# Early expert table and first expert weights in the routing block, and PE adding the gated rows in the last stage

## The reference, cut to what matters

```python
logits = (t @ w_router + b_router)
top_vals, top_idx = lax.top_k(logits, 4)
probs = jax.nn.softmax(top_vals)
order = argsort(flat_e)                       # token rows sorted by expert
gu = ragged_dot(xs, w_gu, group_sizes) + b_gu[e_sorted]
out = ragged_dot(act, w_down, group_sizes) + b_down[e_sorted]
ffn = einsum('tkd,tk->td', slots, probs)
x = layer_norm(DN_ALPHA * x + g2 * ffn, ln2_g, ln2_b)
```

## Time and profile before

| | us |
|---|---|
| runs of the kernel before (3) | 6109.48, 6113.31, 6122.75 |
| median | 6113.31 |
| profiled execution, its time | 6120.77 |
| profiled execution, its span | 6119.2 |
| PE busy in it | 5785.5 (95%) |
| DVE busy | 4270.6 (70%) |
| routing block, from DVE's first instruction (L1711) to its last (L1794) | 3089.6 to 3162.4 |
| experts, POOL's first copy to PE's last product | 3163.8 to 5999.5 |
| last stage, first DMA issue to the end of the span | 6011.2 to 6119.2 |

### The profile page before, as it was taken

The page is one execution under the profiler, slowest core; times in us unless marked ns, Lnnn a source line. Parts: engine busy times, 40 slices in busy tenths (PEclk is TensorE's granted clock), DMA queues, the critical chain, the costliest instruction groups (busy, mean ns, idle before and its releaser), DMA issues. The chain is left out here.

```text
span 6119.2 us, 78464 instructions
## 1 busy us (share of the span) xinstructions
PE 5785.5 (95%) x27512; PEld 4699.9 (77%) x27512; DVE 4270.6 (70%) x3430; ACT 3157.2 (52%) x2883; POOL 1033.3 (17%) x751
## 2 busy tenths in 40 slices
PE   5899999998999989998959999999999999999995
PEld 2688888886777768886748888888888888888882
DVE  3333300224566565554779999999999999999996
ACT  5222211003444444442337777777777777777772
POOL 1000000002333320001511111111111111111112
PEclk7899999999999999999969999999999999999997
DMA  5311212113444445554329553315468359532455
GB/s 224 119 72 72 79 72 74 46 41 102 132 137 133 136 159 186 183 187 149 128 117 357 170 187 120 120 31 199 150 218 328 123 210 408 212 93 58 139 189 186
DMA packets 298555, 924.56 MB, mean 151 GB/s; under 512 B 25808, under 2 KB 163280, under 8 KB 260368
## 3 DMA queue, kind: packets, MB, share of 16 engines
q1 hardware_dynamic: 207696, 701.59, 31.1%
q0 software_dynamic: 40800, 170.84, 9.9%
q10 hardware_dynamic: 49920, 50.34, 2.4%
HBM read 744.27 MB, written 178.54 MB: 151 GB/s over the span
## 5 line engine op out<-in xcount | busy, mean ns | idle before, releaser
L2012 DVE TENSOR_TENSOR moe_w_lo<-moe_w_gu,moe_w_hi 128x2048 fp32r<-128x2048 f32 x648 | 1441.0, 2287 | 3.0 <-ACT moe_w_hi L1958 3.0
L1958 ACT CAST moe_w_hi<-moe_w_gu 128x2048 fp32r<-128x2048 f32 x648 | 1238.7, 1912 | 378.0 <-PE moe_ps_gu L1901 191.4
L2018 DVE TENSOR_TENSOR moe_w_lo<-moe_w_dn,moe_w_hi 128x2048 fp32r<-128x2048 f32 x324 | 734.2, 2288 | 31.8 <-ACT moe_w_hi L1968 31.8
L1968 ACT CAST moe_w_hi<-moe_w_dn 128x2048 fp32r<-128x2048 f32 x324 | 620.2, 1915 | 256.2 <-PE moe_ps_gu L1901 256.2
L1901 PE MATMUL moe_ps_gu<-moe_w_hi,moe_hT_hi 128*128 128x512 f32 x2592 | 702.6, 393 | 12.3 <-DVE moe_w_lo L2012 12.3
L166 PE MATMUL prj_ps_p<-h_hi,prj_w_hi 128*128 128x512 f32 x1792 | 698.5, 390 | 15.7 <-DVE prj_w_lo L537 15.7
L166 PE MATMUL prj_ps_p<-h_hi,prj_w_lo 128*128 128x512 f32 x1792 | 698.1, 390 | 0.0
L166 PE MATMUL prj_ps_p<-h_lo,prj_w_hi 128*128 128x512 f32 x1792 | 698.1, 390 | 0.0
L1901 PE MATMUL moe_ps_gu<-moe_w_lo,moe_hT_hi 128*128 128x512 f32 x2592 | 694.4, 390 | 0.0
L1901 PE MATMUL moe_ps_gu<-moe_w_hi,moe_hT_lo 128*128 128x512 f32 x2592 | 694.0, 390 | 0.0
L1901 PEld LDWEIGHTS moe_ps_gu<-moe_w_lo,moe_hT_hi 128*128 128x128 f32 x2592 | 487.8, 188 | 101.8
(11 more groups left out here) (322 smaller groups left out, 9553.2 us busy)
## 6 DMA issues: line engine op xcount, KB each, us to landing
moe_w_gu<-in_w_gu_t SPq DMA_DIRECT2D x128, 2048.0 KB, 11.0
moe_w_dn<-in_w_down_t SPq DMA_DIRECT2D x64, 2048.0 KB, 9.6
rows_scratch<-prj_out POOLq DMA_DIRECT2D x48, 1024.0 KB, 4.4
brn_w<-in_w_branch_t SPq DMA_DIRECT2D x64, 768.0 KB, 6.8
prj_w<-in_w_in_t SPq DMA_DIRECT2D x80, 512.0 KB, 4.3
moe_b_gu<-b_gu_scratch SPq DMA_DIRECT2D x32, 1024.0 KB, 8.8
nin_w<-in_w_ada SPq DMA_DIRECT2D x24, 1024.0 KB, 8.0
rows_scratch<-ssd_out ACTq DMA_DIRECT2D x96, 256.0 KB, 2.9
```

Source lines behind the costliest of these rows:

```text
L1958: act.copy(w_hi[n % NB][:], raw(w_gu, n)).then_inc(gu_hi, 1)
L1968: act.copy(w_hi[(GU + n) % NB][:], raw(w_dn, n)).then_inc(dn_hi, 1)
L2012: dve.tensor_tensor(w_lo[n % NB][:], raw(w_gu, n), w_hi[n % NB][:].bitcast(F32), ALU.subtract).then_inc(gu_lo, 1)
L2018: dve.tensor_tensor(w_lo[b][:], raw(w_dn, n), w_hi[b][:].bitcast(F32), ALU.subtract).then_inc(dn_lo, 1)
```

## The change

It has two parts.

**In the routing block**: rank and counts are read where they lie in PSUM. The expert of each tile is worked out right behind `cum`: partition c counts the experts whose running sum is at most c (128x32), and PE turns that column into a row with the identity. `S.expert` is written before the picks, on one partition. SP, which had nothing to do in this block, reads the first expert and issues the four transfers of its gate and up weights there; `w_gu` and its semaphores are allocated ahead of the block, and `fetch_gu(0)` in the experts' block returns at once. The four products of `hot` become one of four times the size.

```diff
-                pe.wait_ge(iotas, 6)
+                pe.wait_ge(iotas, 7)
                 pe.wait_ge(chosen_ready, 1)
                 rhs = chosen[:].rearrange("p t e -> p (t e)")
                 pe.matmul(psR[:], strict[:], rhs, start=True, stop=True)
                 pe.matmul(psC[:], S.ones[:], rhs, start=True, stop=True).then_inc(ranked, 1)
+                pe.wait_ge(owned, 1)
+                pe.matmul(psE[0:1, 0:P], te_col[:], S.ident[:], start=True, stop=True).then_inc(owners, 1)
...
+
+            @block.sync
+            def _(sp):
+                sp.wait_ge(tabled, 1)
+                apart(sp, S)
+                first = sp.value_load(S.expert[0:1, 0:1], min_val=0, max_val=E - 1)
+                for c, dst in enumerate(S.w_gu):
+                    sp.dma_start(dst[:], A["w_gu_t"][bass.ds(first * GU_ROWS + c * P, P), :]).then_inc(S.gu_in[c], 16)
...
-                chain.step(dve.tensor_copy(rank[:].rearrange("p t e -> p (t e)"), psR[:]))
-                chain.step(dve.tensor_copy(count[:].rearrange("p t e -> p (t e)"), psC[:]))
                 chain.step(dve.memset(base[:, 0, :], 0.0))
                 for t in range(TT):
-                    chain.step(dve.tensor_tensor(base[:, t + 1, :], base[:, t, :], count[:, t, :], ALU.add))
+                    chain.step(dve.tensor_tensor(base[:, t + 1, :], base[:, t, :], psC[:, t * E:(t + 1) * E], ALU.add))
...
-                chain.step(dve.tensor_tensor(place[:], rank[:], base[:, 0:TT, :], ALU.add))
+                chain.step(dve.tensor_scalar(cmp[:], cum[a][:], iota_c[:, 0:1], None, ALU.is_le))
+                chain.step(dve.tensor_reduce(te_col[:], cmp[:], AX.X, ALU.add))
+                dve.tensor_scalar(te_col[:], te_col[:], float(E - 1), None, ALU.min).then_inc(owned, 1)
+                chain.step(dve.tensor_tensor(place[:], psR[:].rearrange("p (t e) -> p t e", e=E), base[:, 0:TT, :], ALU.add))
                 chain.step(dve.tensor_tensor(place[:], place[:], tiles[:].unsqueeze(1).to_broadcast([P, TT, E]), ALU.add))
-                for k in range(TOPK):
-                    chain.step(dve.tensor_tensor(hot[:, :, k, :], hot[:, :, k, :], place[:], ALU.mult))
+                dve.wait_ge(owners, 1)
+                chain.step(dve.tensor_copy(S.expert[0:1, :], psE[0:1, 0:MOE_COLS]))
+                dve.sem_inc(tabled, 1)
+                chain.step(dve.tensor_tensor(hot[:], hot[:], place[:].unsqueeze(2).to_broadcast([P, TT, TOPK, E]), ALU.mult))
...
-                chain.step(dve.tensor_tensor(cmp[:], iota_t[:].unsqueeze(2).to_broadcast([P, MOE_COLS, E]),
-                                             cum[a][:].unsqueeze(1).to_broadcast([P, MOE_COLS, E]), ALU.is_ge))
-                chain.step(dve.tensor_reduce(te[:], cmp[:], AX.X, ALU.add))
-                chain.step(dve.tensor_scalar(te[:], te[:], float(E - 1), None, ALU.min))
-                chain.step(dve.tensor_copy(S.expert[:], te[:]))
-
+                chain.step(dve.tensor_copy(te[:], psE[0:1, 0:MOE_COLS]))
                 chain.step(dve.memset(fresh[:, 0:1], 1.0))
                 chain.step(dve.tensor_tensor(fresh[:, 1:], te[:, 1:], te[:, :MOE_COLS - 1], ALU.not_equal))
-                chain.step(dve.tensor_copy(S.fresh[:], fresh[:]))
+                chain.step(dve.tensor_copy(S.fresh[0:1, :], fresh[:]))
...
-        w_gu = [sb(f"w_gu{k}", [P, CHUNK * U]) for k in range(GL)]
+        w_gu = S.w_gu
...
-        gu_in, dn_in = sems("moe_gu_in", GL), sems("moe_dn_in", DL)
+        gu_in, dn_in = S.gu_in, sems("moe_dn_in", DL)
...
                 def fetch_gu(i):
+                    if isinstance(i, int) and i == 0:
+                        return
                     fetch(i, [(w_gu[c], lambda e, c=c: A["w_gu_t"][bass.ds(e * GU_ROWS + c * P, P), :], gu_in[c],
                                gu_lo, GU * (i - 1) + CHUNK * (c + 1)) for c in range(GL)])
...
+        S.w_gu = [sb(f"w_gu{c}", [P, D * 2 * FF // GU_ROWS]) for c in range(GU_ROWS // P)]
+        S.gu_in = sems("gu_in", len(S.w_gu))
         route(nc, A, S, sem, sems)
         experts(nc, A, S, sem, sems)
         combine(nc, A, S, sem, sems, out)
```

```diff
-        psT = ps("dense", [E3, SEQ])
-        psB = [ps(f"rest{i}", [P, D]) for i in range(2)]
...
+        sums = ps("sums", [P, B * D])
+        psT = sums[0:E3, 2 * D:2 * D + SEQ]
+        psB = [sums[:, i * D:(i + 1) * D] for i in range(B)]
...
                 def load_x1(t):
                     wait(sp, rested, t - R + 1)
                     apart(sp, S)
-                    sp.dma_start(x1[t % R][:], S.x1_d[t * P:(t + 1) * P, :]).then_inc(x1_in[t % R], 16)
+                    sp.dma_start(x1[t % R][:], S.x1_d[t * P:(t + 1) * P, :]).then_inc(row_in[t % R], 16)
 
                 def load_acc(t):
-                    wait(sp, scaled, t - R + 1)
+                    wait(sp, taken, t - R + 1)
                     apart(sp, S)
-                    sp.dma_start(acc[t % R][:], S.sum_d[t * P:(t + 1) * P, :]).then_inc(acc_in[t % R], 16)
+                    sp.dma_start(acc[t % R][:], S.sum_d[t * P:(t + 1) * P, :]).then_inc(row_in[t % R], 16)
...
                 for t in range(TT):
-                    wait(pe, added, t - 1)
-                    pe.wait_ge(x1_in[t % R], 16 * (t // R + 1))
+                    if t == 2:
+                        pe.wait_ge(dense_ready, 2)
+                    wait(pe, normed, t - B + 1)
+                    pe.wait_ge(row_in[t % R], 32 * (t // R + 1))
                     for c in range(D // BANK):
                         cols = slice(c * BANK, (c + 1) * BANK)
-                        pe.matmul(psB[t % 2][:, cols], alpha[:], x1[t % R][:, cols], start=True, stop=False)
+                        last = pe.matmul(psB[t % B][:, cols], alpha[:], x1[t % R][:, cols], start=True, stop=False)
+                    last.then_inc(rested, 1)
+                    pe.wait_ge(gated, t + 1)
+                    for c in range(D // BANK):
+                        cols = slice(c * BANK, (c + 1) * BANK)
+                        last = pe.matmul(psB[t % B][:, cols], S.ident[:], acc[t % R][:, cols], start=False, stop=False)
+                    last.then_inc(taken, 1)
                     if t == 0:
                         pe.wait_ge(dense_ready, 2)
                         pe.wait_ge(bdn_ready, 3)
                     for c in range(D // BANK):
                         cols = slice(c * BANK, (c + 1) * BANK)
-                        last = pe.matmul(psB[t % 2][:, cols], d_part[:, t * P:(t + 1) * P], b_part[:, cols], start=False, stop=True)
-                    last.then_inc(rested, 1)
+                        pe.matmul(psB[t % B][:, cols], d_part[:, t * P:(t + 1) * P], b_part[:, cols], start=False, stop=True).then_inc(added, 1)
...
                 def normalise(t):
                     act.wait_ge(shifted, t + 1)
-                    act.activation(acc[t % R][:], acc[t % R][:], ACT.Identity, bias=nb[t % Y][:], scale=rs[t % Y][:]).then_inc(normed, 1)
+                    wait(act, stored[t % Y], 16 * (t // Y))
+                    act.activation(yo[t % Y][:], psB[t % B], ACT.Identity, bias=nb[t % Y][:], scale=rs[t % Y][:]).then_inc(normed, 1)
...
                 def gate(t):
-                    dve.wait_ge(acc_in[t % R], 16 * (t // R + 1))
+                    dve.wait_ge(row_in[t % R], 32 * (t // R + 1))
                     dve.tensor_tensor(acc[t % R][:], acc[t % R][:], g2[:], ALU.mult).then_inc(gated, 1)
 
                 def blend(t):
                     s = t % Y
-                    dve.wait_ge(gated, t + 1)
-                    dve.wait_ge(rested, t + 1)
-                    dve.tensor_tensor(acc[t % R][:], psB[t % 2][:], acc[t % R][:], ALU.add).then_inc(added, 1)
-                    dve.wait_ge(added, t + 1)
                     for half in range(2):
-                        dve.bn_stats(st[s][:, half, :], acc[t % R][:, half * BANK:(half + 1) * BANK]).then_inc(halves, 1)
+                        dve.wait_ge(added, 2 * t + half + 1)
+                        dve.bn_stats(st[s][:, half, :], psB[t % B][:, half * BANK:(half + 1) * BANK]).then_inc(halves, 1)
...
                 def scale(t):
                     dve.wait_ge(normed, t + 1)
-                    wait(dve, stored[t % Y], 16 * (t // Y))
                     if t == 0:
                         dve.wait_ge(ln_in, 32)
-                    dve.tensor_tensor(yo[t % Y][:], acc[t % R][:], lg[:], ALU.mult).then_inc(scaled, 1)
+                    dve.tensor_tensor(yo[t % Y][:], yo[t % Y][:], lg[:], ALU.mult).then_inc(scaled, 1)
...
                 gate(0)
+                gate(1)
                 for t in range(TT + 1):
                     if t < TT:
                         blend(t)
-                    if t + 1 < TT:
-                        gate(t + 1)
+                    if t + 2 < TT:
+                        gate(t + 2)
                     if t < TT:
                         invert(t)
                     if t > 0:
```

24 lines of the change are left out of this document (14 added, 10 removed).

## The result

| | before | changed |
|---|---|---|
| median of the runs, us | 6116.2 (6 runs, 6109.48 to 6122.75) | 6096.19 (6 runs, 6088.15 to 6098.51) |
| profiled execution, its time | 6120.77 | 6095.71 |
| its span | 6119.2 | 6094.0 |

The ratio of the runs is 0.9965, with a 95% interval of 0.9955 to 0.9975: the changed kernel is faster by 20.0 us, where 21.1 were predicted. (Before was run again beside the changed kernel, so its median is a little above the 6113.3 of the first three runs.)

A forecast was written before the change was run, and what follows sets the result against it. PE was busy 95% of the span, so only places where it waits could give. Gains of 7.6 + 6.2 + 7.3 = 21.1 us took the profiled 6120.8 to 6099.7, or the median 6113.3 to 6092.2; range 6077 to 6103.

The forecast's parts named there:

- Routing block: DVE's chain in the routing block: 9.6 us removed, 2.0 added, net gain 7.6 us, bounds 7.0 and 9.
- Start of the experts: First gather, issue to turned rows, takes 6 us with the weights transferred early; gain 6.2 us, bounds 0 and 8.1.
- Rival B: Start of the experts: gather stays late because bias and down weights replace gate and up weights; total gain 15, 6098; chance 0.11.
- Last stage: Addition taken off DVE, gating held until POOL ends: 4.94 us per tile; gain 7.3 us, bounds 0 and 20.
- 0.4 us of DVE's wait: Last stage, each tile: this wait for POOL becomes visible as a long gating of some 1.8 us.
- Rival A: Last stage: POOL does not hold up the gating, tile 4.06 us; stage gains some 20, total 34, 6079; chance 0.07.
- the last two tiles: Last stage: no gating left; about 3.7 instead of 5.3 us for one, about 0.9 gained on the last; together 2.5.
- the twelve tiles: Last stage: tiles of the regular form take 4.94 us each, a gain of 0.37 apiece, 4.4 us together.
- both are covered, with 0.7 us and a tenth to spare: Last stage: PE's 3.9 to 4.2 us per tile and DMA's 318 GB/s, against 352 full, fit under 4.94 us.
- Rival C: Last stage gives nearly nothing: loads come late for the gating or first tiles wait for PE; total 14, 6099; chance 0.11.
- Rival D: Last stage: PE stays at 1.2 GHz, tile about 8 us, stage 43 us more; net loss of 29, 6142; chance 0.03.
- Rival E: Early transfers: expert known no earlier or transfers wait at the barrier; gain only 15 us, 6098; chance 0.02.

The follow-up runs named there:

- experiments 1 and 2: Changed kernel with one part alone: routing block and early weights, last stage as before, 6102.67 us; or only the last stage changed (PE adds gated rows), 6110.80 us.
- experiment 4: Changed kernel, but SP asks for the bias and down weights only once the first gathered rows have landed: 6095.76 us, ratio 0.9967 against before.
- experiment 3: Changed kernel with the early transfers of the first expert's weights put back in the experts' block, shorter routing chain kept: 6102.85 us, ratio 0.9978 against before.
- experiment 5: Changed kernel without POOL's addition of ln_b in the last stage, POOL only signalling: 6085.15 us (one run).
- experiment 8: Changed kernel with the last stage's scaling put ahead of the gating, so that the gating begins before POOL: 6112.76 us (one run).
- experiment 9: Changed kernel, last stage rearranged: ACT normalises in PSUM, DVE scales from PSUM, one-tensor-input tiny product, gating behind scaling, six result tiles: 6081.65 us, ratio 0.9943 against before.
- experiment 1: Changed kernel with only the routing block and early weights changed, last stage as before: 6102.67 us, ratio 0.9979 against before.
- Experiments 6 and 7: Changed kernel with ring loads waiting for the scaling, so they cannot run ahead: 6094.63 us; or with six result tiles instead of four: 6094.70 us.

## Why the prediction was right

**The sum: 21.1 us predicted, 20.0 measured.** Its three terms came out at 8.5, 5.9 and 5.6 against 7.6, 6.2 and 7.3. The mechanisms of all three were right, but the closeness of the total is partly luck: the errors have both signs, and the last term is known to a microsecond or two only (experiments 1 and 2).

**Routing block, 8.5 instead of 7.6.** What is removed was right, 9.6. What is added was put at 2.0 and is 1.17: the three small steps 0.56 (0.66), the two copies 0.69 (0.6), and the additions from PSUM -0.08, where 0.8 was taken. That last value came from a pair of rows, 0.26 from PSUM against 0.21 from SBUF on 128x100; it did not carry over to the chained 128x32 steps. The Trainium skill's figures ("Perfetto Trace Analysis", section "Optimizing Scalar/DVE Operations"), which gave 1.0 for this term, do not show in these additions either, and the measurement decides: the 16 additions took 3.59 us from SBUF and 3.51 from PSUM, and `bn_stats` on 128x512 has a mean of 687 ns from PSUM against 686 from SBUF. The lower bound of the prediction, 0, is what happened.

**Start of the experts, 5.9 of 6.2.** The 6 us, put together from the median of 5.0 and one more for the bias, met 6.34 (5.95 to 6.38 in the eight profiles with the early transfers and without experiment 4's edit), and experiment 3 shows that the transfers alone make it. The parts of it were off and made up for each other: with nothing beside it the gather took 4.37, and bias and down weights together cost 2.0. Rival B, a gather that stays late, fell: 5 MB asked for within 4 us of it cost 2.0 us (experiment 4), 8 MB and the bias had cost 7.9 (12.28 against 4.37). The weights were issued at 3113.8 and landed by 3135. The step behind it held as well: from turned rows to first product 7.29 us in both kernels, and the expert loop passed the shift on.

**Last stage, 5.6 instead of 7.3.** The pattern was right to 0.02 us: 4.92 for the predicted 4.94, with the gating ending 1.08 us behind POOL. (The "0.4 us of DVE's wait" and the gating of "some 1.8" do not follow from the prediction's own counts: from 1.6 to 3.52 the gating takes 1.9, 0.8 more than its 1.17. Measured: 2.03, 0.86 more.) Experiment 5 shows that POOL is the cause and what would be without it, 4.05 (predicted 4.06). This is the Trainium skill's rule of an exclusive lock on the ports ("SBUF — State Buffer", section "SBUF: two separate sides"), and the runs agree with it in both directions: DVE is held by POOL (2.03 for 1.17, 2.12 for 0.16) and, as experiment 8 reads it, POOL by DVE (3.26 for 2.35). Rival A therefore fell, but the 20 us that it offered were nearly there: experiment 9 frees DVE in another way and has a last stage of 87.8, 20.2 us below before and 18.9 below the same stage in experiment 1.

Of the terms, the last two tiles gave 2.8 (1.73 and 1.10, from the distances 3.59 and 3.57 for 5.32 and 4.67) for the predicted 2.5, the start 0.0 for 0.4, and the twelve tiles 2.8 for 4.4. Those 2.8 hold the 2.1 us lost in the two long tiles, and 0.4 won from the one slow tile of before. At the start no gain of 0.4 shows in any profile of the changed stage: from the bias's arrival to the first scaling it is 15.4 us with the old code (twice) and 15.2 to 16.1 with the new. **The step that failed** is the one on the DMA engines, "both are covered, with 0.7 us and a tenth to spare". It compared a mean, 318 GB/s, with what I took for full, 352. The engines can do more, 409 to 425 GB/s in the windows above, but what they were asked for was not the mean. The change also moved the point at which ring tiles come free, from the scaling to PE's reading (for `x1` the wait was on PE before as well, but SP issued it behind the one for `acc`), and so gave the loads leave to run at PE's 3.9 us a tile instead of DVE's 4.9, and to fill the engines. It moved the wait for the store as well, from the scaling to ACT's normalisation ahead of it, in the chain of the same tile. Both lines stand in the diff and were not priced. Experiments 6 and 7 show that the long tiles come from these; with them away the stage gains 8.2 to 8.4 us against the profile of before, 6.8 to 7.0 against the same stage in experiment 1. Rival C had the right resource and the wrong victim: it spoke of loads late for the gating, and the loads were early; the stores were late.

**Rival D, the low clock,** fell entirely. The granted clock, 0.83 in one window before, is 1.00 in all windows of 15 us from 6010 to 6070. PE had more work and less waiting, and its loads stood 0.43 us apart. **Rival E** fell with the row of 3113.77, where the transfers are issued 36 us ahead of the block's end, and with experiment 3.

**What the forecast owed its place to** was that the removed addition was not taken at its 1.25 us a tile. In the rows of before the gating looks free, 1.17 us; that it only stood clear of POOL by its order was read from two other places, where DVE ended 1.09 us behind POOL. Without that the last stage's gain would have been put at some 20 us, and the total 13 too high.
